# The gate step ahead of the transposes in one core's attention program

## What is computed

```python
q_a, kv_a, gate_a, qkv_b, q_c, kv_c, merge = split_cols(h @ w_in, IN_WIDTHS)
o_a = nsa_attention(...)       # 8 heads: compressed, selected blocks ("slc"), window of 512 ("win")
o_b = stick_breaking(...)      # 4 heads ("sb")
o_c = swa_with_sinks(...)      # 4 heads, window of 128 ("swa")
g = jax.nn.sigmoid(merge).reshape(B, S, N_BRANCH, D)
y = g[:, :, 0] * (o_a @ w_branch_a) + g[:, :, 1] * (o_b @ w_branch_b) + g[:, :, 2] * (o_c @ w_branch_c)
```

## Time and profile before

| what | value |
|---|---|
| median of 3 runs (lowest to highest) | 1787.11 us (1783.25 to 1788.55) |
| the profiled execution | 1787.33 us |
| its span, first to last instruction | 1785.5 us |
| mean granted TensorE clock | 0.969 |
| attention, from the first scores to the last values | about 338 to 1091 us of the span |
| TensorE matmuls | 8573, busy 94% |

### The profile page before, as it was taken

One profiled execution on the slowest core, in us unless ns is written; L12 is line 12 of the kernel. 1 busy time (PEld: TensorE's weight loads), 2 busy tenths in 40 slices (PEclk: granted clock), 3 DMA queues, 4 the chain that ended last, 5 costly groups with the idle time before them and its releaser, 6 DMA issues.

```text
span 1785.5 us, 23790 instructions
## 1 busy us (share of the span) xinstructions
PE 1672.9 (94%) x8573; PEld 1302.6 (73%) x8573; DVE 1024.2 (57%) x1665; ACT 732.8 (41%) x1272; POOL 364.4 (20%) x342
## 2 busy tenths in 40 slices
PE   6999999699999999999999988999939999999996
PEld 5555464477778778888878877888828888888885
DVE  5564442535465555566565565775485565656485
ACT  1421110344545545545455553331133544545473
POOL 2211133000000001101020110000022434346355
PEclk9999999699999989999999989999959999999998
DMA  9415360032222111121111113752266887878794
GB/s 339 151 47 188 118 165 24 13 95 71 71 72 72 53 37 54 54 54 54 36 54 36 42 54 118 282 189 106 99 244 188 271 268 260 270 258 298 239 376 125
DMA packets 146955, 247.68 MB, mean 139 GB/s; under 512 B 6424, under 2 KB 69984, under 8 KB 145536
## 3 DMA queue, kind: packets, MB, share of 16 engines
q1 hardware_dynamic: 138544, 217.81, 35.8%
q0 software_dynamic: 8112, 27.93, 6.5%
q10 hardware_dynamic: 192, 0.54, 0.1%
HBM read 210.60 MB, written 36.18 MB: 138 GB/s over the span
## 4 chain that ended last, share of the span: by engine, by line
PE 80%; DVE 9%; DMA 4%; issue 3%; ACT 3%; POOL 1%; SPq 0%; ACTq 0%; DVEq 0%; POOLq 0%
PE psum L1866 10%; PE psum L2032 7%; PE psum L1970 5%; PE psum L2211 5%; PE psum L2212 5%; PE psum L2216 5%; PE psum L2000 5%; PE psum L1886 3%; PE psum L2254 2%; PE psum L2255 2%; PE psum L2259 2%; DMA arena<-in_w_in_dram 2%; PE psum L2049 2%; PE psum L2063 2%; PE psum L2066 2%
## 5 line engine op out<-in xcount | busy, mean ns | idle before, releaser
L805 POOL TENSOR_SCALAR arena<-arena 128x128 f32<-128x128 f32 (+7 forms) x32 | 71.1, 2222 | 667.9 <-ACT arena L1057 352.3
L2032 PE MATMUL psum<-kv,arena 128*128 128x64 f32 x1464 | 192.1, 275 | 2.2 <-ACT arena L422 2.2
L2032 PEld LDWEIGHTS psum<-kv,arena 128*128 128x128 f32 x1464 | 187.0, 198 | 4.9 <-ACT arena L422 2.9
L1866 PE MATMUL psum<-arena 128*128 128x512 f32 (+2 forms) x512 | 189.0, 522 | 0.3 <-DVE arena L1219 0.3
L1469 DVE TENSOR_REDUCE negm<-psum 128x1 f32<-128x640 f32 (+7 forms) x128 | 90.2, 705 | 113.1 <-PE psum L1973 112.7
L2211 PE MATMUL psum<-heads_r,kv_r 128*128 128x512 f32 x384 | 150.9, 393 | 3.4 <-DVE kv_r L1736 3.4
L1866 PEld LDWEIGHTS psum<-arena 128*128 128x128 f32 x512 | 95.9, 192 | 77.4 <-issue 73.8
L1730 DVE TENSOR_TENSOR arena_r<-arena,heads_r 128x2048 fp32r<-128x2048 f32 x64 | 142.5, 2287 | 15.1 <-ACT heads_r L1130 15.1
L2212 PE MATMUL psum<-heads_r,kv_r 128*128 128x512 f32 x384 | 150.6, 392 | 0.0
L2000 PE MATMUL psum<-ident,arena 128*128 128x128 f32 x828 | 133.5, 284 | 17.4 <-ACT arena L1030 12.3
L1030 ACT ACTIVATE arena<-psum,negm 128x640 f32<-128x640 f32 (+7 forms) x128 | 89.3, 697 | 135.8 <-DVE negm L1469 135.2
(11 more groups left out here) (441 smaller groups left out, 3468.0 us busy)
## 6 DMA issues: line engine op xcount, KB each, us to landing
arena<-in_w_exp_gate_dram SPq DMA_DIRECT2D x16, 2048.0 KB, 12.0
arena<-in_w_exp_down_dram SPq DMA_DIRECT2D x16, 2048.0 KB, 12.5
arena<-in_w_exp_up_dram SPq DMA_DIRECT2D x16, 2048.0 KB, 13.9
arena<-in_w_in_dram SPq DMA_DIRECT2D x48, 512.0 KB, 4.2
arena<-in_w_ada_dram SPq DMA_DIRECT2D x7, 2048.0 KB, 11.1
z_dram<-arena SPq DMA_DIRECT2D x48, 256.0 KB, 2.3
arena<-z_dram SPq DMA_DIRECT2D x8, 1536.0 KB, 7.5
bc<-in_w_ada_dram SPq DMA_DIRECT2D x4, 2048.0 KB, 8.4
```

Of the source, the lines that this page charges most:

```text
L1866: mm = pe.matmul(psum[:, 4 + s % 3, 0:w], hT[:, k, n * P:(n + 1) * P], slot(slot_of(L_TOK + ch))[:, k, 0:w], start=(k == 0), stop=(k == NK ...
L2032: mm = pe.matmul(psum[:, bank, c * HD:(c + 1) * HD], pt[:, j * P:(j + 1) * P], v, start=(j == 0), stop=(j == u["nb"] - 1))
```

## The change

In slots whose `s["T"]` has one set, the gate step is issued ahead of the transposes, no longer behind everything. Where there are two sets it stays between them. A slot without any set would have it at its end, as before. Nothing else changes, neither on the other engines nor in the DMA queues' programs.

```diff
@@ -2072,7 +2072,7 @@
                     if u is not s["ride"]:
                         scores(u)
                 for j, u in enumerate(s["T"]):
-                    if j == 1:
+                    if j == 1 or len(s["T"]) == 1:
                         gate_matmuls(q)
                     if waiting and "v" not in u:
                         values(waiting)
@@ -2083,7 +2083,7 @@
                     waiting = u if "v" in u else None
                 if s["ride"]:
                     scores(s["ride"])
-                if len(s["T"]) < 2:
+                if not s["T"]:
                     gate_matmuls(q)
             if waiting:
                 values(waiting)
```

## The result

The changed kernel takes 1853.72 us (median of 4 runs, 1851.45 to 1856.77), and the kernel before 1785.18 us beside it (4 runs, 1781.75 to 1788.55). The ratio is 1.0381, with a 95% interval from 1.0364 to 1.0399: 3.8%, or 68 us, slower. The prediction was 1839 us, slower, in a range of 1812 to 1864.

The account below looks back on a forecast made before the run. The prediction took PE, which never waits in tiles 4 to 6, to bound the kernel. Its terms, -2.6 + 20.4 + 14.4 + 10.2 = 42.4 us and 10 for the clock, added 52 to 1787.33: 1839 us, range 1812 to 1864.

Parts of the forecast that it names:

- signs of being wrong: Whole kernel: attention ending before 1110 us, L1057 ending no waits, or idle time growing about 42 us but span quite differently.
- Term 1: Three transposes that waited in changed slots now have a gate step ahead of them: gain 2.6 us.
- Term 2: Scores after 14 rides of tiles 4 to 7 wait for ScalarE's copy (L1057), no longer hidden: loss 20.4 us.
- Term 3: PE waits on VectorE's backlog, once per tile from 1 on (11.5 us) and in smaller places (2.9): loss 14.4 us.
- Term 4: Gate steps c = 0 wait for the copy of the gate bank (L1068), tile 0 put at nothing: loss 10.2 us.
- Term 5: Clock falls to half behind three of some eleven waits of over 1.2 us at full tiles: loss 10 us.
- The cover holds: Rival: backlog and bank's copy end earlier than reckoned, no clock loss; about 1813 us, chance 0.17.
- The clock falls at nearly each wait: Rival: clock costs 27 to 37 us on top of 42.4, giving 1857 to 1867 us; chance 0.16.

Follow-up runs that it names:

- e5: Kernel before, with the gate step moved ahead of the transposes only in the 14 ride slots of tiles 4 to 7: +29.2 us over before, ratio 1.0154.
- e6: Kernel before, with the gate step moved ahead of the transposes only in slots i = 1 (7 tiles): +17.4 us over before, ratio 1.0096.
- e3: Changed kernel, with gate steps c = 0 back at the end in slots with one set: +46.2 us over before, ratio 1.0262.
- e4: Changed kernel, with early gate steps left only in slots with one set, no ride, i other than 1, c = 1 or 2: +11.2 us over before.
- e1: Changed kernel, with the gate step back at the end in the 32 slots with a ride: +45.1 us over before, ratio 1.0252.
- e8: Kernel e4, with tile 7 in the order of before as well: +4.8 us over before, ratio 1.0024.

## Why the prediction was right, and where its sizes were off

**The direction and the mechanisms.** The forecast had PE's waits opened by lost cover, in three places, with the clock as an addition. All three are in the trace at the places named (slots behind rides, i = 3, c = 0), and each is seen alone: rides in e5, VectorE's backlog in e6, the bank's copy by its return in e3. Nothing takes the delay back behind the attention, which ends at 1150.7 us for 1086.1. The sum of the waits was put at 42.4 us with a gain of 2.6 in it, and idle time grew by 33.6.

**The size, and the luck in it.** The waits were put some 9 us too high and the clock some 21 too low, and the two errors partly cancel. With the clock of the runs on top of my waits the sum is 74 us, or 1861; with the measured idle time and my clock it is 44, or 1831. Both lie in the range of 8 in 10, so the range did not hang on the luck, but that 1839 is within 15 us of 1853.72 is partly luck. One of my signs of being wrong, a span that grows by a quite different amount than the idle time, came near: 64.5 against 33.6.

**Term 1**, the gain of 2.6 us. The waits before the three transposes of the earlier trace rows are gone. But L2000's waits on L1030 stayed at 12.6 us in sum, as slots 23 and 43, with two sets, wait 2.1 and 1.2 us longer for VectorE's backlog. In e4, where the backlog is left its cover, these waits are 3.5 us shorter than before.

**Term 2**, 20.4 us behind rides. Measured in the 14 places: 14.9 us of idle time (0.79 to 1.65 each). Ten of them are the bare copy; the backlog that I took over from the old distances for i = 9 and 15 was nearly all hidden. What I missed is slot 152, which has no gate step, but whose wait grew from 1.24 to 2.89 us, as slot 151's step moved away.

**Term 3**, 14.4 us. The waits at i = 3 grew by some 10 us against 11.5; tile 3 has none, where I had one in every tile from 1 on. Of the five smaller places that I put at 2.9 us, two show any wait.

**Term 4**, 10.2 us. L1068's waits rose from 2.6 to 15.5, by 12.9. I had put tile 0's at nothing, and they are there: four waits of 0.8 to 1.1 us.

**Term 5**, the clock at 10 us, is the one term that was badly mis-sized: 31.6 us in the profiled execution. I took the clock to fall behind three of eleven waits of over 1.2 us, from one case each way. The trace of the kernel before had more cases. Beside the two of the earlier trace rows its tiles 1 to 7 have three waits of over 1.2 us, of 2.45, 2.99 and 1.62 us, and half clock follows each:

```profile
632.40:642.60 10.20, 10.20 (x34) 7.57 (x35) 4.25 (x5) 3.61 (x9) 0.00 (x0) 0.50 0.08 24
...
1055.70:1062.40 6.70, 6.70 (x32) 6.18 (x31) 3.86 (x6) 3.35 (x6) 0.00 (x0) 0.50 0.02 4
...
1069.40:1072.70 3.30, 3.30 (x18) 3.30 (x17) 3.27 (x4) 0.15 (x1) 0.00 (x0) 0.50 0.00 0
```

That is four falls behind five waits, and four fifths of the 37 us would have been 30. All four are in slots without a gate step, by which I had set slot 152 apart; in the changed kernel the clock falls in slots with one too, as at 738 us. Shorter waits count as well: in e5 it fell behind six of the 14 waits, all of 0.79 to 1.11 us. What kept the clock up after the 1.41 us of the earlier trace rows was left open, and it still is. Tiles 4 to 7 have narrow matmuls with values around each wait, while the waits of 1.43 us in slots 111, 114 and 117 of the changed kernel, directly ahead of a gate step, are followed by no fall. That is an observation and not a test.

**The rivals.** "The cover holds" at 1813 us is refuted. "The clock falls at nearly each wait", at 1857 to 1867, was nearer to the result than its 0.16 says: the idle time was less than I had reckoned and the clock as that rival had it. The Trainium skill tells, in "TensorE: Matmul & The Clock Gate", "A second HAM failure mode: psum-queue depth-cycling", of a kernel in which frequent micro-idles between groups of matmuls make the clock swing and cost throughput. I had let one wait speak against that as a rule here, and the trace of the changed kernel agrees with it (0.94 of full clock in tiles 4 to 6, 1.00 before), though not every short wait is followed by a fall.

## What to carry to other kernels

A filler that PE can do at any time was worth most here behind the work whose reader frees the next buffer; ask of each place what it covers there, and what stands behind that engine's backlog, before it is moved to where it covers another wait. Where PE never waits in a stage, a new order of its program can only open waits, and each short one is to be priced with the clock that may fall behind it: here the clock's part was as large as the idle time itself. Parts that share cover are not known from being undone one by one. Here they gave 55 us so and 57 together, which looks like a plain sum, but six ride slots were in two of the parts, and e1 still waited where the step of the slot before was early. And one profiled execution says where the clock fell, not how much it costs: in e8 it said 9.2 us, and twelve runs said none.

## What was not expected of the hardware

After 0.79 us of idle time the granted clock was 0.50 for 6.8 us (e5). The runs of one kernel differ by what the clock does: e8's twelve lie between 1785.91 us, at a mean clock of 0.973, and 1796.40, at 0.964. This spread does not follow the number of waits: e3's four runs, with 18 us more idle time than before, lie within 1.3 us. And 52 matmuls that nobody reads made the changed kernel 12 us faster.
